# The first microseconds of a two-block kernel: which load goes first, and what is turned first

## The reference, cut to what matters

```python
def rmsnorm(t, g):
    tf = t.astype(jnp.float32)
    y = tf * lax.rsqrt(jnp.mean(tf * tf, axis=-1, keepdims=True) + NORM_EPS)
    return (y * g.astype(jnp.float32)).astype(t.dtype)
```

## Time and profile before

| | us |
|---|---|
| median of 3 runs | 2381.3 |
| lowest and highest run | 2380.57, 2382.02 |
| the profiled execution | 2380.48 |
| its span in the trace | 2378.9 |
| TensorE busy | 2079.8 (87% of the span) |
| VectorE busy | 1160.4 (49%) |
| ScalarE busy | 437.1 (18%) |

### The profile page before, as it was taken

The page is one execution under the profiler, slowest core; times in us unless marked ns, Lnnn a source line. Parts: engine busy times, 40 slices in busy tenths (PEclk is TensorE's granted clock), DMA queues, the critical chain, the costliest instruction groups (busy, mean ns, idle before and its releaser), DMA issues. The chain is left out here.

```text
span 2378.9 us, 30126 instructions
## 1 busy us (share of the span) xinstructions
PE 2079.8 (87%) x12452; PEld 1432.3 (60%) x12452; DVE 1160.4 (49%) x2277; ACT 437.1 (18%) x906; POOL 51.4 (2%) x65
## 2 busy tenths in 40 slices
PE   7999999997676667666666699999999999999998
PEld 5788888862222222222222258878999459899953
DVE  6999897230011011101110128565877756687764
ACT  2231211120000000000000012351333014333311
POOL 0111110000000000000000000000000000000000
PEclk9999999998878777778787799999999999999999
DMA  8768866799999999999999995443454446544430
GB/s 297 256 144 255 228 187 226 283 381 428 427 428 429 428 428 428 429 429 428 428 429 428 427 404 212 169 151 124 169 178 165 177 140 241 202 169 161 177 142 18
DMA packets 161037, 668.95 MB, mean 281 GB/s; under 512 B 11237, under 2 KB 64014, under 8 KB 131998
## 3 DMA queue, kind: packets, MB, share of 16 engines
q1 hardware_dynamic: 148638, 645.15, 68.6%
q0 software_dynamic: 11008, 16.78, 3.6%
q10 hardware_dynamic: 1280, 5.44, 0.6%
HBM read 666.27 MB, written 17.86 MB: 288 GB/s over the span
## 5 line engine op out<-in xcount | busy, mean ns | idle before, releaser
L1776 PE MATMUL PS<-arena,hT 128*32 128x512 f32 x2048 | 317.9, 764 | 150.5 <-DMA arena<-in_w_up_dram 112.6
L1776 PEld LDWEIGHTS PS<-arena,hT 128*32 128x32 f32 x2048 | 66.7, 128 | 379.7 <-DMA arena<-in_w_up_dram 189.4
L1830 PE MATMUL PS<-arena,hT 128*32 128x512 f32 x1008 | 169.1, 807 | 96.4 <-DMA arena<-in_w_down_dram 90.6
L1413 PE MATMUL PS<-hT,arena 128*128 128x256 f32 (+1 forms) x1136 | 247.5, 380 | 0.6 <-ACT hT L845 0.6
L2313 DVE SCALAR_TENSOR_TENSOR arena<-arena 128x512 f32<-128x512 f32 (+2 forms) x514 | 246.4, 547 | 0.8
L2316 DVE TENSOR_TENSOR arena<-arena 128x1024 f32<-128x1024 f32 (+2 forms) x283 | 232.2, 841 | 27.4 <-PE PS L2112 23.1
L2316 DVE TENSOR_TENSOR hT<-hT,PS 128x512 f32<-128x512 f32 x16 | 16.4, 1028 | 464.3 <-PE PS L1776 464.3
L1413 PEld LDWEIGHTS PS<-hT,arena 128*128 128x128 f32 (+1 forms) x1136 | 210.5, 189 | 32.4 <-issue 2.8
L2068 PE MATMUL PS<-hT,arena 128*128 128x128 f32 x1408 | 164.9, 275 | 0.6 <-DVE hT L2316 0.6
L1830 PEld LDWEIGHTS PS<-arena,hT 128*32 128x32 f32 x1008 | 32.9, 130 | 216.2 <-DMA arena<-in_w_down_dram 139.4
L2068 PEld LDWEIGHTS PS<-hT,arena 128*128 128x128 f32 x1408 | 160.9, 192 | 1.0 <-DVE hT L2316 1.0
(11 more groups left out here) (347 smaller groups left out, 2427.9 us busy)
## 6 DMA issues: line engine op xcount, KB each, us to landing
arena<-in_w_gate_dram SPq DMA_DIRECT2D x64, 2048.0 KB, 40.5
arena<-in_w_up_dram SPq DMA_DIRECT2D x64, 2048.0 KB, 41.0
arena<-in_w_down_dram SPq DMA_DIRECT2D x63, 2048.0 KB, 38.5
arena<-in_ffn_w_up_dram SPq DMA_DIRECT2D x32, 2048.0 KB, 8.0
arena<-in_w_in_dram SPq DMA_DIRECT2D x36, 1024.0 KB, 9.0
arena<-in_ffn_w_down_dram SPq DMA_DIRECT2D x16, 2048.0 KB, 7.9
arena<-in_w_ada_dram SPq DMA_DIRECT2D x12, 2048.0 KB, 12.5
arena<-in_ssd_w_in_dram SPq DMA_DIRECT2D x10, 2048.0 KB, 9.9
```

The source lines that it names most:

```text
L1413: mm = pe.matmul(dsts[i % parts], l, r, start=(i < parts), stop=(i >= parts * (n - 1)), skip_group_check=parts > 1)
L1776: mm = pe.matmul(PS[32 * f:32 * f + 32, 1 + half, :], xe[:, 32 * (2 * pi + k):32 * (2 * pi + k) + 32], w[:, k, 512 * f:512 * f + 512], sta ...
L1830: mm = pe.matmul(PS[32 * q:32 * q + 32, 4 + n, :], htr[:, P * q + 32 * pi:P * q + 32 * pi + 32], w[:, q, 512 * n:512 * n + 512], start=(pi ...
```

## The change

SP issues panel 0 of w_ada right behind the constants and in front of the seven groups of rows. Panel 3 is loaded by two DMAs of one chunk each; the first announces itself by the slot's semaphore and the second by extra_in, on which TensorE waits between the two chunks. The count that the last expert waits for on extra_in grows by 16. TensorE turns x first and the rows behind it, and ScalarE copies and squares x before it copies the rows and makes the Silu. The semaphore rows_t therefore counts x's four banks first and the rows fifth.

```diff
             def load_ada(j):
                 g, jj = j // 4, j % 4
+                if j == 3:
+                    dst = at("ada", j, 2, 2048)
+                    load("ada", j, dst[:, 0:1, :], w_ada[:, 6:7, 0:2048])
+                    sp.dma_start(dst[:, 1:2, :], w_ada[:, 7:8, 0:2048]).then_inc(s["extra_in"], 16)
+                    return
                 load("ada", j, at("ada", j, 2, 2048), w_ada[:, 2 * jj:2 * jj + 2, 2048 * g:2048 * g + 2048])
...
             sp.dma_start(const[:, :], A["shape_const"]).then_inc(s["const_loaded"], 16)
+            load_ada(0)
             for piece in PIECES[:EARLY]:
                 sp.dma_start(*row_piece(*piece)).then_inc(s["early_loaded"], 16)
-            for j in range(4):
+            for j in range(1, 4):
                 load_ada(j)
...
-            act.wait_ge(s["rows_t"], 1)
-            cols_copy(0, [0])
-            act.wait_ge(s["cols_ready"], 1)
-            act.activation(condT, cols[:, COL["c"]:COL["c"] + 8], ACT.Silu).then_inc(s["cond_ready"], 1)
             for b in range(4):
-                act.wait_ge(s["rows_t"], b + 2)
+                act.wait_ge(s["rows_t"], b + 1)
                 act.activation(xT_[:, 512 * b:512 * b + 512], PS[:, 2 + b, :], ACT.Copy).then_inc(s["x_ready"], 1)
...
             squares("mix1", x_piece, lambda p: ("x_ready", p + 1))
+            act.wait_ge(s["rows_t"], 5)
+            cols_copy(0, [0])
+            act.wait_ge(s["cols_ready"], 1)
+            act.activation(condT, cols[:, COL["c"]:COL["c"] + 8], ACT.Silu).then_inc(s["cond_ready"], 1)
             root("mix1")
...
             pe.wait_ge(s["const_loaded"], 16)
-            pe.wait_ge(s["early_loaded"], 16 * EARLY)
-            rows_turn(0, [0])
             pe.wait_ge(s["x_loaded"], 32)
...
                 if d % 2:
                     mm.then_inc(s["rows_t"], 1)
+            pe.wait_ge(s["early_loaded"], 16 * EARLY)
+            rows_turn(0, [0])
             square_sum("mix1", sq)
...
                     k = 2 * jj + kk
+                    if j == 3 and kk:
+                        pe.wait_ge(s["extra_in"], 16)
                     for q in range(4):
...
                     if last and pi >= 2:
-                        pe.wait_ge(s["extra_in"], 32)
+                        pe.wait_ge(s["extra_in"], 48)
```

## The result

The changed kernel takes 2383.8 us (median of 22 runs, 2381.88 to 2384.49) against 2380.74 us for the kernel before (22 runs, 2379.04 to 2382.26): a ratio of 1.0012, 95% interval 1.0006 to 1.0017. It is slower by 3.1 us at the medians, less than the 0.2% that the chances were given for. The profiled execution took 2384.18 us with a span of 2382.4; the span before was 2378.9.

A forecast was written before the change was run, and what follows sets the result against it. Bound: the first projection's start, behind panel 3's landing. x at 14.4 + 19.5 TensorE work + 0.3 = 34.2 us against 32.38, +1.8; 2381.3 + 1.8 = 2383.1, given as 2383.0; range 2379.0 to 2385.5.

The forecast's parts named there:

- slow start: TensorE's first work on x, no longer preceded by the rows' transpose: slow weight loads cost 0.3 us, about 0.4 at most.
- The load order: Loads at the start: panel 0 shares the engines one packet for one, x 4.5 us late (0 to 5.0).
- 2.98 us of slack: TensorE behind x: its waits for panels 2 and 3, 0.79 + 2.19 us, can absorb lateness of x.
- The halves: Panel 3 in two loads: nothing with x late; at most about 0.65 us if its landing stays the bound, capped by mla_in.
- The new order of turning: Turning, copying and squaring x ahead of the rows on TensorE and ScalarE: gain 0.
- The stream of panels: Panel loads with panel 0 issued 2.9 us earlier: 0.3 us gain less about as much for the rows' packets, sum 0.
- Rival A: Loads at the start: x gets through before panel 0 takes its share, gain 0.65 to 1.5 us, time 2380.3; chance 23%.
- B: DMA queues: panel 0 goes in runs of 16 packets, x needs two turns, 10 us late, +7.3 us, 2388.6; chance 6%.
- C: After the first projection: the +1.8 us is lost in a later wait, or x's delay equals the slack; 2381.3; chance 9%.

The follow-up runs named there:

- e1: Kernel before with only the new load order, panel 0 of w_ada issued in front of the rows; ratio to before 1.0011.
- e4: Changed kernel with x's two loads issued by SP between the constants and panel 0, no longer by ScalarE; ratio to before 1.0003.
- e3: Kernel before with only panel 3 loaded in two halves; ratio to before 0.9999.
- e9: Kernel before without the two groups of four filler matmuls behind panels 1 and 2; ratio to before 0.9996.
- e2: Kernel before with only the new order of turning, copying and squaring, all loads as before; ratio to before 1.0001.
- e7: Changed kernel with ten early fillers before x lands and without the eight behind panels 1 and 2; ratio to before 1.0004.
- e6: Changed kernel without the two groups of four filler matmuls behind panels 1 and 2; ratio to before 0.9998.
- e8: Changed kernel with only the first half (1 MB) of panel 0 in front of the rows, the second behind them; ratio to before 1.0008.
- e11: Kernel before with panel 3 in two loads, two more fillers between its halves' matmuls, and mla_in in two loads; ratio to before 1.0002.
- e10: Kernel before with panel 3 in two loads and two more filler matmuls between the halves' matmuls; ratio to before 0.9999.
- e12: Changed kernel without the eight fillers behind panels 1 and 2 and with mla_in in two loads; 2378.85 us, ratio to before 0.9990.

## Why the prediction was right, and where it was off

It named 2383.0 us for a measured 2383.8, in the range and on the right side, and the cause was what it said. That the two lie so close is in part luck: the forecast shift was +1.8 us and the measured one is +3.1, but the runs of before had a median of 2380.74 beside this result where the forecast started from 2381.3. The range's upper end was also reckoned too high: a delay of 5.0 and a slow start of 0.4 give +2.4, not +2.7, so 2384.7 and not 2385.0. Point by point:

- **The load order doesn't bring the stream forward, it makes x late by 4.5 us.** Right: 4.65 us, with 0.13 MB/us for x where 0.14 was worked out. e1 isolates it, e4 takes it away.
- **TensorE has 2.98 us of slack.** Right: both waits for w_ada are gone. From panel 0's start to panel 3's end it took 11.19 us, and 14.31 before; 0.14 us less than the sum without the waits.
- **The slow start costs 0.3 us, at most 0.4.** This is the term that failed. It was sized for the transposes only. From x to panel 0 it is 25.00 - 14.56 = 10.44 us against 8.16, 2.28 more: 0.34 up to the start of the squares and 1.94 in the squares, which I had taken at full rate. The 0.34 has the size foreseen but not the cause given: e3 and e9, with the rows' transpose still first, need 4.88 us from x to the squares, the changed kernel 4.85 and the trace of before 4.51, where the clock came up while x was being turned (12.59 us). In some executions the 1.94 is absent; the sum 4.65 + 0.34 - 2.98 - 0.14 = +1.87 us then is the forecast's +1.8, and the lower group of runs lies 1.1 to 2.0 us above before's median.
- **The halves bring nothing here, and 0.65 us at most alone.** Right at the projection (0.72 us in e3, released by mla_in), too high at the end, where 0.16 us was left at the first mark. "What comes through" had to be followed over the next 40 us, not only to the next landing.
- **The new order of turning is worth nothing.** Right on the old loads (e2's time), wrong on the new ones: e1's projection is 1.1 us later without it, since the rows then land behind x.
- **The stream of panels gains nothing.** Right: the last part of panel 3 is released at 30.60 us with the new load order (e7) and 30.46 with the old, and where it comes a microsecond earlier it does so with either order, at 29.57 (e6) and 29.47 (e9). That microsecond has a reason that I hadn't listed (below).
- **Rival A** (x keeps its place) and **B** (runs of 16 packets) fall with x at 14.56 us and with 16 packets against 17 in half a microsecond. The Trainium skill's whole packets of 9 to 17 descriptors ("DMA: Bandwidth & Descriptors", "Queues, rings and completion order") are not what these records show: here two queues alternate one for one. **C** (absorbed on the way) falls with 3.82 us against 3.83 at the first mark.

## What to carry to other kernels

When a load is issued earlier on an already full set of DMA engines, ask whose bytes it takes: a small load on the other queue got one packet for one here, so its share was set by the ratio of the packet sizes, a third for 4 KB against 8 KB, and half the competing bytes in front did not halve its delay (e8). Count the slack of the engine behind it, and price that engine's restart at the low clock for everything it does there, not only for its first instructions. Fillers are free only while the engine would have waited: they cost 3.6 us once x was late (e6), and without them the clock fell in the traces in which TensorE was ahead of the loads (e7, e9).

## What was not expected of the hardware

**An instruction fetch seems to delay a landing.** In the traces of before, e2, e3, e7 and e11 the last part of panel 3 is released at 30.39 to 30.60 us, in e9 at 29.47 and e6 at 29.57. Between 27 and 30 us before has a packet of the instruction queue among the others, and e9 has none:

```profile
q1 hardware_dynamic: 483, 1.12, 96.4%
q8 instruction: 1, 0.02, 2.3%
```
```profile
q1 hardware_dynamic: 489, 1.15, 99.7%
```

2.3% of 16 engines over 3 us are 1.1 us of one engine, and the panel would wait for that engine. All five traces with the later landing have such a packet between 27 and 30 us, and the two with the earlier one don't: theirs stands between 33 and 34 us (e9) and between 30 and 31 (e6). That this is the cause is read from this agreement, not tried by itself.

**Waits for instructions.** At about 70 us TensorE stood still with the mark "issue" for 0.24 us before and for 1.20 to 3.44 us in six others (e3, e4, e7, e8, e10, e11); the rest show no such wait. Whether it is a late instruction fetch stays open.

**The clock.** With the same program and the same arrival of x the sum of squares took 5.66, 5.65 and 3.72 us (after, e12, e6), as the first grant of the upper level came at 23.36, 23.44 or 18.64 us; PEclk reads 1.00 in all of them, so at a kernel's start the rate of the records has to be looked at. And waits of 2.08 and 2.45 us in front of panel 3 were followed by a granted clock of 0.50 (e2, e7) where one of 2.19 us (before) was not. Which of them happens in an execution stays open; it moves this kernel by some 2 us.
